# A transformer block in fp32: the last block of x normalised by two engines in halves, and the last head pair's gate multiplied in ahead of the norm's factor

## The reference

```python
h = rmsnorm(x, norm1_g)                  # x * rsqrt(mean(x*x) + 1e-6) * g
z = h @ w_in                             # 1024 -> 3328 (rwkv) + 1536 (qkv) + 2048 (gates)
y_a = rwkv7_time_mix(z_rwkv, ...) @ w_proj_a
y_b = window_sink_attention(q, k, v, sink) @ w_proj_b
x = x + (g_a * y_a + g_b * y_b) @ w_out
x = x + conv_ffn(rmsnorm(x, norm2_g), ...)
return rmsnorm(x, normf_g)
```

```python
y = (y - mean) * rsqrt(var + 64e-5)      # per token and head
y = y * lnx_w + lnx_b
y = (y + bonus) * g                      # g = sigmoid(zg) @ g2
```

## Time and profile before

| | |
|---|---|
| median of 3 runs | 1044.11 us (1043.87 to 1044.27) |
| the profiled execution | 1044.27 us, span 1042.2 us |
| mean granted TensorE clock | 0.998 |
| TensorE busy | 1026.7 us, 99% |
| DVE busy | 737.3 us, 71% |
| ScalarE busy | 514.3 us, 49% |
| GpSimd busy | 218.2 us, 21% |

### The profile page before, as it was taken

The page is one execution under the profiler, slowest core; times in us unless marked ns, Lnnn a source line. Parts: engine busy times, 40 slices in busy tenths (PEclk is TensorE's granted clock), DMA queues, the critical chain, the costliest instruction groups (busy, mean ns, idle before and its releaser), DMA issues.

```text
span 1042.2 us, 17905 instructions
## 1 busy us (share of the span) xinstructions
PE 1026.7 (99%) x6640; PEld 824.5 (79%) x6640; DVE 737.3 (71%) x1226; ACT 514.3 (49%) x865; POOL 218.2 (21%) x290
## 2 busy tenths in 40 slices
PE   8999999999999999999999999999999999999997
PEld 7888888777687777877777888888888888888886
DVE  5225667587988878788777455367777777789786
ACT  6435776544445445354553333265454544557744
POOL 8532246220211312213130434300000000000000
PEclk9999999999999999999999999999999999999999
DMA  7874466330303314133333876804233333336663
GB/s 200 241 211 142 133 232 203 113 72 21 85 24 72 73 45 113 35 81 84 122 77 109 248 245 207 276 23 116 87 100 101 93 99 91 100 111 219 204 190 115
DMA packets 161287, 133.20 MB, mean 128 GB/s; under 512 B 32729, under 2 KB 137735, under 8 KB 161223
## 3 DMA queue, kind: packets, MB, share of 16 engines
q1 hardware_dynamic: 147552, 88.37, 29.0%
q0 software_dynamic: 13520, 43.90, 13.6%
q10 hardware_dynamic: 151, 0.04, 0.0%
HBM read 111.83 MB, written 20.45 MB: 127 GB/s over the span
## 4 chain that ended last, share of the span: by engine, by line
PE 96%; DVE 2%; DMA 1%; issue 1%; ACT 0%; SPq 0%; DVEq 0%; ACTq 0%
PE ps L1995 15%; PE ps L1997 15%; PE ps L1998 15%; PE ps L1951 5%; PE ps L1953 4%; PE ps L1952 4%; PE ps L2522 3%; PE ps L2524 3%; PE ps L2523 3%; PE ps L2158 3%; PE ps L2285 2%; PE ps L2306 2%; PE ps L2101 1%; PE ps L2457 1%; PE ps L2456 1%; PE ps L2458 1%
## 5 line engine op out<-in xcount | busy, mean ns | idle before, releaser
L1286 DVE TENSOR_TENSOR wlo<-raw,whi 128x1024 fp32r<-128x1024 f32 x108 | 142.1, 1316 | 132.3 <-ACT whi L832 114.5
L832 ACT ACTIVATE whi<-raw 128x1024 fp32r<-128x1024 f32 x116 | 122.6, 1057 | 133.8 <-PE ps L1998 124.0
L1998 PE MATMUL ps<-xnh,wlo 128*128 128x512 f32 x336 | 130.9, 390 | 0.0
L1995 PE MATMUL ps<-xnh,whi 128*128 128x512 f32 x336 | 130.9, 389 | 0.0
L1997 PE MATMUL ps<-xnl,whi 128*128 128x512 f32 x336 | 130.9, 389 | 0.0
L1995 PE MATMUL ps<-xh,whi 128*128 128x512 f32 x240 | 94.7, 395 | 1.1 <-DVE xl L1304 1.1
L1997 PE MATMUL ps<-xl,whi 128*128 128x512 f32 x240 | 93.6, 390 | 0.0
L1998 PE MATMUL ps<-xh,wlo 128*128 128x512 f32 x240 | 93.5, 390 | 0.0
L1951 PE MATMUL ps<-xh,whi 128*128 128x512 f32 x184 | 85.2, 463 | 0.4 <-DVE wlo L1286 0.4
L1997 PEld LDWEIGHTS ps<-xnl,whi 128*128 128x128 f32 x336 | 63.1, 188 | 13.1
L1995 PEld LDWEIGHTS ps<-xnh,whi 128*128 128x128 f32 x336 | 63.1, 188 | 13.1
(11 more groups left out here) (401 smaller groups left out, 2461.1 us busy)
## 6 DMA issues: line engine op xcount, KB each, us to landing
raw<-in_w_in SPq DMA_DIRECT2D x108, 256.0 KB, 3.1
raw<-in_w_up SPq DMA_DIRECT2D x88, 256.0 KB, 3.0
wrow<-in_w_down POOLq DMA_DIRECT2D x22, 512.0 KB, 4.9
raw<-weight_scratch SPq DMA_DIRECT2D x44, 256.0 KB, 3.4
raw<-in_w_down SPq DMA_DIRECT2D x32, 256.0 KB, 2.9
weight_scratch<-wrow POOLq DMA_DIRECT2D x11, 512.0 KB, 3.3
gates_scratch<-gst POOLq DMA_DIRECT2D x16, 256.0 KB, 3.3
raw<-in_w_proj_b SPq DMA_DIRECT2D x16, 256.0 KB, 4.1
```

Of the source, the lines that this page charges most:

```text
L832: act.activation(flat(whi[:, hb]), flat(raw[:, b]), ACT.Copy).then_inc(w_hi, 1)
L1286: dve.tensor_tensor(flat(lo[:, hb]), flat(raw[:, b]), flat(hi[:, hb]).bitcast(F32), ALU.subtract).then_inc(w_lo, 1)
L1995: pe.matmul(ps[bank][:, :], whi[:, hb, k, :], hi(k), start=first and k == 0, stop=False)
L1998: ins = pe.matmul(ps[bank][:, :], wlo[:, hb, k, :], hi(k), start=False, stop=last and k == kn - 1)
```

## The change

Two things change. In the norm of x the fourth block is handled in halves of 512 features. ScalarE squares and sums the left half, DVE the right half (`scalar_tensor_tensor` with `accum_out`, into a scratch tile `junkx`), and DVE adds 1e-6 to its sum, which becomes the bias of ScalarE's square root (signal `x_part`). After the reciprocal DVE scales the left half and ScalarE the right half (signal `x_half`, for which TensorE waits ahead of the fifth tile of that block). ScalarE's half scaling stands ahead of its first weight split.

For the last pair, (y f + b + bonus) g is computed as (y g) f + (b + bonus) g, f being the norm's factor. DVE makes (b + bonus) g inside the scan (`gated_bonus` at (3, "z")), and `last_output` multiplies by the gate before it waits for the factor. TensorE turns the factor ahead of the low products 2 and 3 of `tb` and not behind them.

```diff
--- before.py
+++ after.py
@@ -203,6 +203,7 @@
         xt = at(ZR, "xt", [P, NT, D])
         junk = at(QR, "junk", [P, D])
         rows = at(QR + 4 * K, "rows", [P, 3, P])
+        junkx = at(QR + 6 * K, "junkx", [P, T])
 
 
         take = taker(WR, arena_bytes)
@@ -329,6 +330,8 @@
         par_ready = sem("par_ready")
         x_sq = sem("x_sq")
         x_inv = sem("x_inv")
+        x_part = sem("x_part")
+        x_half = sem("x_half")
         g1_ready = sem("g1_ready")
         x_scaled = sem("x_scaled")
         x_t = sem("x_t")
@@ -864,7 +867,7 @@
 
             act.wait_ge(consts, 1)
             table(ACT.Sqrt)
-            for j in range(NT):
+            for j in range(NT - 1):
                 if j == 2:
                     act.wait_ge(par_t, 1)
                     act.activation(par[:, 0:KT], ps[7][:, 0:KT], ACT.Copy).then_inc(g1_ready, 1)
@@ -875,6 +878,15 @@
                     lo = 0 if j == 1 else j
                     act.activation(stat[:, 4 + lo:5 + j], stat[:, lo:j + 1], ACT.Sqrt,
                                    scale=1.0 / D, bias=eps_col[:, 0:1]).then_inc(x_sq, 1)
+            act.wait_ge(x_in[NT - 1], 16)
+            chain(act.activation(junk[:, 0:T], xt[:, NT - 1, 0:T], ACT.Square,
+                                 accum_out=stat[:, 3:4]))
+            act.wait_ge(x_part, 1)
+            act.activation(stat[:, 7:8], stat[:, 3:4], ACT.Sqrt, scale=1.0 / D,
+                           bias=stat[:, 13:14]).then_inc(x_sq, 1)
+            act.wait_ge(x_inv, 3)
+            act.activation(xt[:, NT - 1, T:D], xt[:, NT - 1, T:D], ACT.Copy,
+                           scale=stat[:, 11:12]).then_inc(x_half, 1)
             split(0, 0, 0, first=True)
 
             act.wait_ge(g1_ready, 1)
@@ -1291,11 +1303,19 @@
 
 
             for i, (lo, hi) in enumerate(((0, 2), (2, 3), (3, 4))):
+                if i == 2:
+                    dve.wait_ge(x_in[NT - 1], 16)
+                    chain(dve.scalar_tensor_tensor(junkx[:, :], xt[:, NT - 1, T:D], 1.0 / D,
+                                                   xt[:, NT - 1, T:D], ALU.mult, ALU.mult,
+                                                   accum_out=stat[:, 12:13]))
+                    dve.tensor_scalar(stat[:, 13:14], stat[:, 12:13], 1e-6, None, ALU.add)\
+                        .then_inc(x_part, 1)
                 dve.wait_ge(x_sq, i + 1)
                 dve.reciprocal(stat[:, 8 + lo:8 + hi], stat[:, 4 + lo:4 + hi]).then_inc(x_inv, 1)
                 dve.wait_ge(x_inv, i + 1)
                 for j in range(lo, hi):
-                    dve.tensor_scalar(xt[:, j, :], xt[:, j, :], stat[:, 8 + j:9 + j], None,
+                    cols = slice(0, T if j == NT - 1 else D)
+                    dve.tensor_scalar(xt[:, j, cols], xt[:, j, cols], stat[:, 8 + j:9 + j], None,
                                       ALU.mult).then_inc(x_scaled, 1)
             split(0, 0, 0)
             dve.wait_ge(g1_ready, 1)
@@ -1472,16 +1492,14 @@
                 chain(dve.tensor_tensor(ysb[:, :], ysb[:, :], ps[6][:, :], ALU.mult))
 
             def with_bonus(d):
-                product = tile(d + 8) if d < PAIRS - 1 else bp[:, :]
-                if d < PAIRS - 1:
-                    dve.wait_ge(product_ready, d + 1)
-                chain(dve.scalar_tensor_tensor(ysb[:, :], ysb[:, :], pcol("lb", d), product,
+                dve.wait_ge(product_ready, d + 1)
+                chain(dve.scalar_tensor_tensor(ysb[:, :], ysb[:, :], pcol("lb", d), tile(d + 8),
                                                ALU.add, ALU.add))
 
-            def gated(d, bank=5):
+            def gated(d):
 
                 dve.wait_ge(gmul_ps, d + 1)
-                dve.tensor_tensor(tile(d), ysb[:, :], ps[bank][:, :], ALU.mult)\
+                dve.tensor_tensor(tile(d), ysb[:, :], ps[5][:, :], ALU.mult)\
                     .then_inc(pair_done, 1)
 
             def weights(n):
@@ -1649,12 +1667,25 @@
                 value_tokens(n)
                 invert(n, n - 1, n < PAIRS - 1)
 
+            def gated_bonus(d):
+                dve.wait_ge(gmul_ps, d + 1)
+                dve.scalar_tensor_tensor(bp[:, :], bp[:, :], pcol("lb", d), ps[3][:, :],
+                                         ALU.add, ALU.mult)
+
+            def last_output(d):
+                dve.wait_ge(y_scaled, d + 1)
+                chain(dve.tensor_tensor(ysb[:, :], ysb[:, :], ps[3][:, :], ALU.mult))
+                dve.wait_ge(rstd_ps, d + 1)
+                chain(dve.tensor_tensor(ysb[:, :], ysb[:, :], ps[6][:, :], ALU.mult))
+                dve.tensor_tensor(tile(d), ysb[:, :], bp[:, :], ALU.add).then_inc(pair_done, 1)
+
             def y_lo_of(dst, src, hi, order):
                 dve.wait_ge(yh_ready, order + 1)
                 lo_part(dst, src, hi, yl_ready, 1)
 
             scan(PAIRS - 1, {("first",): [lambda: weights(N_PROJ + 1)],
                              (0, "u"): [lambda: add_bonus(PAIRS - 1)],
+                             (3, "z"): [lambda: gated_bonus(PAIRS - 1)],
                              (0, "s"): [lambda: y_lo(0, 0, 3)],
                              (1, "u"): [lambda: y_lo(0, 1, 4)],
                              (1, "s"): [lambda: y_lo(0, 2, 5)],
@@ -1666,9 +1697,7 @@
             y_lo(1, 1, 1)
             y_lo(1, 2, 2)
             deviations(PAIRS - 1)
-            scaled_output(PAIRS - 1)
-            with_bonus(PAIRS - 1)
-            gated(PAIRS - 1, 3)
+            last_output(PAIRS - 1)
             weights(N_PROJ + 2)
             y_lo_of(yal[:, 7, :], z[:, 7, :], yah[:, 7, :], 8)
 
@@ -2009,6 +2038,8 @@
             for j in range(NT):
                 pe.wait_ge(x_scaled, j + 1)
                 for k in range(KT):
+                    if j == NT - 1 and k == KT // 2:
+                        pe.wait_ge(x_half, 1)
                     ins = pe.transpose(ps[k][:, j * P:(j + 1) * P], xt[:, j, k * P:(k + 1) * P],
                                        ident[:, :])
                     if j == NT - 1:
@@ -2422,10 +2453,13 @@
             pe.wait_ge(yl_ready, 4)
             for k in (6, 7):
                 tb.low(k)
-            for k in range(4):
-                pe.wait_ge(yl_ready, 6 + k // 2)
+            pe.wait_ge(yl_ready, 6)
+            for k in range(2):
                 tb.low(k)
             deviations(PAIRS - 1)
+            pe.wait_ge(yl_ready, 7)
+            for k in range(2, 4):
+                tb.low(k)
             pe.wait_ge(yl_ready, 8)
             tb.low(4)
             tb.low(5, True)
```

## The result

| | before | changed |
|---|---|---|
| median of 12 runs | 1044.12 us (1043.85 to 1045.54) | 1047.07 us (1045.24 to 1048.38) |
| the profiled execution | 1044.27 us, span 1042.2 | 1047.20 us, span 1045.2 |

The ratio is 1.0024 with a 95% interval of [1.0015, 1.0032]: slower by 3 us, outside the range of the prediction. The twelve runs of the changed kernel lie on two levels: three between 1045.24 and 1045.65, nine between 1046.87 and 1048.38. The mean granted clock is 0.999 in the three and 0.995 to 0.998 in the nine. The lower level is the forecast of 1045.2. The upper one is the rival that had been given 4%, the clock.

What follows compares the result with a forecast made beforehand. TensorE, busy for 99% of the span, was taken as the bound, so only its waits at the start and last pair mattered: +1.7 - 0.6 = +1.1 us, median 1045.2, range 1044.3 to 1046.1 (within 0.2%: 90%).

Steps and rivals of the forecast that it cites:

- the forecast of 1045.2: Whole kernel: the predicted median time, 1.1 us above the kernel before; forecast with its bounds given 70%.
- the rival that had been given 4%, the clock: Before the first product: longer TensorE idleness halves the granted clock, costing 5.5 us at the most; 4%.
- The start, +1.7: Before the first product: ScalarE's queue delays `whi` to 12.55, first product to about 15.65; +1.7 us, bounds 1.5 to 2.0.
- The dear sum: DVE's half square at the start: an operation with a sum takes twice 0.75 us, start +2.4, total 1045.9; 6%.
- 0.75 that the prediction had named as a sign of being wrong: DVE's half square at the start: a sum out not later than 0.75 us after its start would count against the prediction.
- The last pair, -0.6: Last pair's tail: `yah` starts at 565.65 instead of 566.30, behind ScalarE's `whi`; -0.6 us, bounds -0.3 to -0.8.
- rows 12: Profile rows at the kernel's end: granted clock 1.00 through 1037 to 1039 without matmuls, 0.50 from 1039 on.
- The sign that had been named for it, a clock of 0.50: At the start: a stretch at a granted clock of 0.50 around 14 us would show the prediction wrong.
- 24 matmuls at double time: First product: all its 24 matmuls at twice their 0.23 us, 5.5 us more at the most, up to 1050.7.
- The free start: Start: new work hides behind the first weights' landing until 10.78, leaving only -0.6, 1043.5; 8% with later partial absorption.
- The tail's gain: Last pair: predicted -0.6 us; the rival that the tail gives nothing (+1.7, 1045.8) had 12%.
- The sum of the two parts, +1.1: Whole kernel: +1.7 at the start and -0.6 at the last pair give +1.1 us, bounds +0.7 and +1.7.

Runs made afterwards that it cites:

- run 6: The changed kernel with ScalarE's half scaling behind the first weight split instead of ahead of it: 1044.65 us median, ratio 1.0004.
- run 2: The changed kernel with x squared and scaled as before, so only the last pair's change: 1043.83 us median against 1044.35, ratio 0.9995.
- run 7: The kernel before with only DVE's part of the last pair's change, TensorE's turning left behind the low products: 1043.69 us against 1044.33.
- run 8: The kernel before with only TensorE's part of the last pair's change, DVE's three steps in the old order: 1043.85 us against 1044.41.
- run 5: The kernel before with one more ScalarE copy of 1024 columns ahead of its first weight split: 1046.57 us median, ratio 1.0016.
- run 1: The changed kernel with the last pair's code put back, so only the norm of x in halves: 1047.29 us median, ratio 1.0024.
- run 10: The kernel before with DVE's part of the last pair's change and one fp32 matmul of 256 columns before the first product: 1043.66 us against 1044.41.
- run 4: The changed kernel with two long fp32 matmuls filling TensorE's idleness ahead of turning the last eighth of x: 1045.43 us against 1044.33.
- run 9: The kernel before with both parts of the last pair's change and one fp32 matmul of 256 columns before the first product: 1043.65 us against 1044.33.
- run 3: The changed kernel with sixteen short turnings of the identity ahead of the last turning of x: 1046.85 us median of 9, ratio 1.0023.

## Why the prediction was wrong

*The start, +1.7.* Right to 0.02 us: first product at 15.63 for 15.65 (the steps as given add up to 15.68), by the chain that was given. The dear sum did not come: DVE's half square took 0.69 with a read of 0.08 that overlaps it, so the whole was out 0.69 after the start, against 0.85 in the sum. (That there are two rows is as the Trainium skill says, page "VectorE: DVE Perf Modes", section "Two Vector instructions with no wait between them".) The 0.69 is under the 0.75 that the prediction had named as a sign of being wrong. Of these 0.16, 0.08 went again into the addition and the hand-overs behind it (0.29 from the sum to the square root, for 0.21), so two small errors cancel in part, and that the end is right to 0.02 is partly luck. ScalarE's half scaling took its 0.6. Run 6 shows the step that carries the loss: of the 1.7, 0.9 is gone when `whi` is put ahead of the half scaling.

*The last pair, -0.6.* The mechanism was right, ScalarE's `whi` is next and behind it the tile's `wlo`. The size was 0.45 in the trace and 0.5 to 0.6 in the medians of runs 2, 7 and 8: `wlo` was 0.16 late and not just in time, and the matmul that waited for it took 0.1 more. It stayed inside the bounds.

*The clock.* **The step that failed** is this one: "It decides only if the gap reaches the idleness that rows 12 show ahead of the fall, and mine is shorter. 4%." It took the idleness at the kernel's end, where TensorE ran nothing for some 3 us before the clock fell (1035.9 to 1039), as the least that is needed for a fall. The runs show falls behind 1.83 us of idleness (run 5), 2.10 (the changed kernel, run 1), 2.07 (run 10) and 2.22 (run 2), partly when TensorE was already at work again. By the levels of the times that is so in 8 of 11 executions each of runs 1 and 5 and in 9 of 12 of the changed kernel, in two of 11 at the most behind 0.88 (run 6), and in none of 11 where the gap is filled (run 4). A level does not say at which place the clock fell, but the kernel before lies above 1045 in only 11 of 85, so the place ahead of x can't make up these numbers. The sign that had been named for it, a clock of 0.50, did come, at 16.4 and not around 14. The price was oversized as well: 24 matmuls at double time had been the bound, and about 8 ran so (1.6 us) in the profiled run, or 13 to 14 (2.7 us) in that of run 1. With the rival at its measured frequency the likeliest time would have been 1045.2 + 1.6 = 1046.8. What was left out of the reckoning is that rows 12 are one gap in one execution, at whose end TensorE had no more work. They show that the clock can hold through 2.3 us of idleness, not that it does so every time, and the longest idleness between two pieces of TensorE's work at a clock of 1.00 was 1.06, less than half of the 2.3 that were forecast. A page of the Trainium skill had been cited for just this risk ("TensorE: Matmul & The Clock Gate", "Part 1: The HAM clock gate"), and the traces agree with it: idleness brings the lower clock.

*The rivals.* The free start did not come. The tail's gain is real: the interval of each of runs 2 and 7 to 10 takes in no change, but all five medians lie 0.5 to 0.8 below the kernel before, and the rows of runs 7 and 8 show 0.5. The sum of the two parts, +1.1, is what run 4 measures (1045.43 against 1044.33) and what the three lower runs of the changed kernel show (1045.24 to 1045.65).

What stays open: why the fall comes in some executions and not in others with the same gap, and how much the shorter gaps ahead of x (1.24 us in run 5, 0.88 and 0.81 in run 1) add to it. Run 3's explanation, that the moved fetch of code delayed the write of the key norms, rests on the two coming together in its profile and on run 4, where neither does; the fetch was not moved by itself.

## What to carry to other kernels

Splitting a step over two engines pays only if the step is on the chain; here x was beside it, and the half given to ScalarE was put ahead of the weight split that everything waited for. When a change makes TensorE's idleness longer, count a fall of the granted clock as a cost of its own, unless gaps as long are followed by work at the full clock in every execution you have: here a delay of 1.7 us cost 3.3 in most executions, and one gap of 3 us through which the clock had held did not rule that out. If such a gap can't be removed, fill it and look at what the added instructions move: two long matmuls cost nothing here, sixteen short turnings came with 1.3 us of waiting elsewhere.

## What the runs showed of the hardware that was not expected

The granted clock fell behind idleness of 1.83 to 2.22 us in five profiles (the changed kernel, runs 1, 2, 5 and 10), and held behind up to 1.43 in the others' starts. In two of the five it fell only after TensorE had been at work again for 0.8 to 1.4 us (at 16.4 in the changed kernel, by the 0.72 of the stretch of 16 to 17, and at 16.7 in run 5). It stayed low for 3.4 us in both, and for 6.8 in run 1. With sixteen added turnings early in the program TensorE waited 1.3 us at 221 us, beside a 16 KB fetch of code that had moved from 5.9 to 0.6 us behind the issue of a 64 KB write, and that write landed in 2.9 us in place of 1.8.
